# Log-and-exp roots, reordered vector work and full-array identity products in a one-core encoder layer

## What is computed

```python
def _rwkv7_step(S, inp):
    r, w, k, v, a, b = inp
    Sa = jnp.einsum('zbhvk,zbhk->zbhv', S, a)
    S = S * w[..., None, :] + Sa[..., :, None] * b[..., None, :] + v[..., :, None] * k[..., None, :]
    return S, jnp.einsum('zbhvk,zbhk->zbhv', S, r)
...
kk = kk / jnp.maximum(jnp.sqrt(jnp.sum(kk * kk, axis=-1, keepdims=True)), 1e-12)
...
yn = ((y - mu) * lax.rsqrt(var + GN_EPS)).reshape(B, T, C) * ln_g + ln_b
```

## Time and profile before

| | |
|---|---|
| median of three runs | 1827.98 us |
| the profiled execution, its own time | 1829.13 us |
| its span | 1827.3 us |
| TensorE busy | 1716.3 us, 94% |
| VectorE busy | 586.4 us, 32% |
| ScalarE busy | 353.9 us, 19% |
| GpSimd busy | 63.1 us, 3% |
| mean granted TensorE clock | 0.989 |

### The profile page before, as it was taken

How to read it: one execution, slowest core, us unless ns; L and a number is a source line. 1 busy time by engine, 2 the same in 40 slices (tenths; PEclk the granted TensorE clock), 3 DMA queues, 4 the chain that set the end, 5 groups by cost and what they waited for, 6 DMA issues and landing times.

```text
span 1827.3 us, 37340 instructions
## 1 busy us (share of the span) xinstructions
PE 1716.3 (94%) x16231; PEld 1096.9 (60%) x16231; DVE 586.4 (32%) x1302; ACT 353.9 (19%) x945; POOL 63.1 (3%) x97
## 2 busy tenths in 40 slices
PE   8999999988989999999899999999999999999997
PEld 7887888867777445676545545454544444544443
DVE  2001333578886201022132322313132222222234
ACT  2122222267665201023100000000000000000002
POOL 1000000000000000002000000000000000000000
PEclk9999999999999999999999999999999999999999
DMA  9933353200000844328799999999999999999993
GB/s 308 206 110 101 110 165 138 92 4 4 4 4 5 297 164 177 130 113 301 291 426 430 429 429 430 431 432 427 433 428 433 428 433 427 433 428 430 429 419 148
DMA packets 95843, 503.65 MB, mean 276 GB/s; under 512 B 37869, under 2 KB 42369, under 8 KB 76913
## 3 DMA queue, kind: packets, MB, share of 16 engines
q1 hardware_dynamic: 90872, 488.17, 66.6%
q0 software_dynamic: 4608, 13.08, 2.4%
q10 hardware_dynamic: 248, 0.65, 0.1%
HBM read 511.29 MB, written 4.23 MB: 282 GB/s over the span
## 4 chain that ended last, share of the span: by engine, by line
PE 69%; DMA 22%; DVE 6%; issue 2%; ACT 1%; DVEq 0%; POOL 0%; SPq 0%; POOLq 0%; ACTq 0%
PE ps L1550 14%; PE ps L2067 8%; PE ps L2191 8%; PE ps L2056 8%; DMA ring<-in_wd 7%; DMA ring<-in_wu 7%; DMA rest<-in_wu 7%; PE ps L1874 6%; PE ps L2075 4%; PE ps L1892 2%; PE ps L1943 2%; PE ps L1960 2%; PE ps L1901 2%; PE ps L2047 1%; PE ps L1763 1%
## 5 line engine op out<-in xcount | busy, mean ns | idle before, releaser
L1550 PE MATMUL ps<-wide,ring 128*128 128x256 f32 x1248 | 275.3, 379 | 1.2 <-PE ps L1550 0.9
L1550 PEld LDWEIGHTS ps<-wide,ring 128*128 128x128 f32 x1248 | 239.0, 195 | 39.7 <-issue 10.1
L1410 DVE TENSOR_TENSOR tokA<-tokA,ps 128x512 f32<-128x512 f32 x256 | 158.5, 681 | 100.5 <-PE ps L2075 100.5
L2067 PE MATMUL ps<-ring,wide 128*64 128x256 f32 x1512 | 172.6, 387 | 16.8 <-DMA ring<-in_wu 16.6
L2191 PE MATMUL ps<-ring,gg 128*64 128x512 f32 x768 | 175.4, 598 | 2.3 <-DMA ring<-in_wd 1.6
L2056 PE MATMUL ps<-ring,wide 128*64 128x256 f32 x1536 | 173.0, 383 | 2.4 <-DVE wide L1398 2.4
L1423 DVE SCALAR_TENSOR_TENSOR gg<-ps,tmp,gg 128x256 f32<-128x256 f32 x32 | 15.5, 484 | 477.5 <-PE ps L2067 477.5
L2067 PEld LDWEIGHTS ps<-ring,wide 128*64 128x64 f32 x1512 | 110.5, 140 | 76.7 <-DMA ring<-in_wu 21.8
L2056 PEld LDWEIGHTS ps<-ring,wide 128*64 128x64 f32 x1536 | 109.8, 138 | 56.8 <-DVE wide L1398 4.0
L2075 PE MATMUL ps<-wide,gg 64*128 64x512 f32 x512 | 135.3, 627 | 0.9 <-ACT wide L824 0.8
L2191 PEld LDWEIGHTS ps<-ring,gg 128*64 128x64 f32 x768 | 50.9, 136 | 120.7 <-issue 111.9
(11 more groups left out here) (376 smaller groups left out, 2064.5 us busy)
## 6 DMA issues: line engine op xcount, KB each, us to landing
ring<-in_wg SPq DMA_DIRECT2D x23, 4096.0 KB, 28.6
ring<-in_wu SPq DMA_DIRECT2D x23, 4096.0 KB, 31.0
ring<-in_wd SPq DMA_DIRECT2D x22, 4096.0 KB, 32.0
rest<-in_wd SPq DMA_DIRECT2D x8, 4096.0 KB, 30.5
ring<-in_w_in SPq DMA_DIRECT2D x7, 4096.0 KB, 15.5
rest<-in_wu SPq DMA_DIRECT2D x7, 4096.0 KB, 29.7
rest<-in_wg SPq DMA_DIRECT2D x7, 4096.0 KB, 29.6
ring<-in_w_out SPq DMA_DIRECT2D x4, 4096.0 KB, 17.4
```

Source lines behind the costliest of these rows:

```text
L1410: V.tensor_tensor(fin_part(t, h, n), fin_part(t, h, n), ps[:, banks[q][h], :], ALU.add).then_inc(S["added"], 1)
L1550: ins = mm(ps[0:rows_, m % 2, 0:T], lhs, hnT[:, k, :], start=k == 0, stop=k == KD - 1)
L2067: ins = mm(ps[CAP * h:CAP * h + CAP, 1, 0:T], xT[:, k, CAP * i:CAP * i + CAP], w[:, T * h:T * h + T], start=k == 0, stop=k == KD - 1)
```

## The change

The diff has four parts.

1. Every `1/sqrt(v)` becomes `exp(-0.5 * ln(v))` on ScalarE, two activations on the same table, which is loaded by hand (`log_and_exp`). VectorE's reciprocals and its steps `v/width + eps` fall away, and so do the table switches in the pairs, for the cross-attention and for the router.

```diff
             def key_norm(p):
                 act.wait_ge(S["rw_n2e"], p + 1)
-                A(ew[:, SQ], ew[:, SQ], ACT.Sqrt).then_inc(S["rw_nrm"], 1)
+                A(ew[:, SQ], ew[:, SQ], ACT.Ln).then_inc(S["rw_nrm"], 1)
+                act.wait_ge(S["rw_nrm"], 2 * p + 1)
+                A(ew[:, SQ], ew[:, SQ], ACT.Exp, scale=-0.5).then_inc(S["rw_nrm"], 1)
...
             def key_norms(p):
-                dve.wait_ge(S["rw_nrm"], p + 1)
-                dc.add(V.reciprocal(ew[:, SQ], ew[:, SQ]))
+                dve.wait_ge(S["rw_nrm"], 2 * p + 2)
...
             def inverse_std(p):
-                dve.wait_ge(S["rw_std"], p + 1)
-                dc.add(V.reciprocal(VAR, VAR))
+                dve.wait_ge(S["rw_std"], 2 * p + 2)
```

```diff
                 if not last:
-                    A(warm, warm, ACT.Sqrt)
+                    key_norm(p + 1)
...
-                    if n == 9:
-                        if not first:
-                            head_std(p - 1)
-                        if not last:
-                            key_norm(p + 1)
+                    if n == 9 and not first:
+                        head_std(p - 1)
...
-                if next_:
-                    A(warm, warm, ACT.Exp)
-                    act.wait_ge(S["rw_tte"], 4 * p + 1)
-                    for n in range(3):
-                        exponential(p + 2, n)
...
                 if next_:
-                    for n in range(3, 8):
+                    for n in range(8):
                         exponential(p + 2, n)
```

```diff
+                if not last:
+                    key_norms(p + 1)
+                    unit_keys()
+                    products_ar(p + 1, 0)
+                    products_bk(p + 1, 0)
+                    products_out(0)
                 if not first:
                     inverse_std(p - 1)
                     normed_head(p - 1)
-                if not last:
-                    key_norms(p + 1)
-                if not first:
                     gated(p - 1)
                 dc.add(V.tensor_copy(BNS, ew[:, BON]))
                 if not last:
-                    unit_keys()
                     bonus_terms(p + 1)
-                    products_ar(p + 1, 0)
-                    products_bk(p + 1, 0)
-                    products_out(0)
-
+                    products_ar(p + 1, 1)
+                    products_bk(p + 1, 1)
+                    products_out(1)
+
+                dve.wait_ge(S["rw_gnow"], p + 1)
...
-                if not last:
-                    dve.wait_ge(S["rw_gnow"], p + 2)
-                    products_ar(p + 1, 1)
-                    products_bk(p + 1, 1)
-                    products_out(1)
+                if next_:
+                    keys(p + 2)
```

```diff
+    c[:, ID + P:ID + P + CH] = c[:, ID:ID + CH]
...
-                    for e, r, q, o in tiles():
-                        ins = mm(ps[o, 2 * g + e, CH:P], ident[q, q], src[q, g, e, 1, :], start=False, stop=True)
+                    for e in range(2):
+                        same_or_other = cst[:, ID + CH * e:ID + CH * e + P]
+                        ins = mm(ps[:, 2 * g + e, CH:P], same_or_other, src[:, g, e, 1, :], start=False, stop=True)
```

More of the change, by code:

```diff
@@ L443, in _ @@
             pool.memset(warm, 1.0)
+            pool.memset(dprm[:, 38:39], EPS)
             pool.memset(praw[:, :, :], 0.0).then_inc(S["zeroed"], 1)
-            pool.memset(idle, 0.0).then_inc(S["idle_in"], 1)
+            pool.memset(idle, 0.0)
             pool.memset(raw[:, :, 0:1], 0.0)
@@ L592, in _ @@
             lora_out(CT - 1)
+            log_and_exp()
             def pt_out(i):
@@ L616, in exponential @@
                     act.wait_ge(S["rw_gnow"], p)
-                if n == 4 and not now:
+                if n == 0 and not now:
                     act.wait_ge(S["rw_prep"], p)
@@ L775, in _ @@
             rows_turned(7, 2)
-            act.wait_ge(S["var_done"], 5)
-            A(stat(3, 2), stat(3, 1), ACT.Sqrt).then_inc(S["std_done"], 2)
+            std(3, 4, "row_sum", 1)
             for n in ("m_sil", "m_ya", "r_ohtok"):
@@ L842, in _, with last_std @@
                 job(NE // 2 - 1, 1, last=True)
+            def last_std(t):
+                one = slice(t, t + 1)
+                act.wait_ge(S["row_sum"], t + 2)
+                A(stat(5, 2)[:, one], stat(5, 0)[:, one], ACT.Ln, scale=1.0 / D, bias=eps).then_inc(S["ln_done"], 1)
+                act.wait_ge(S["ln_done"], 7 + t)
+                A(stat(5, 2)[:, one], stat(5, 2)[:, one], ACT.Exp, scale=-0.5).then_inc(S["std_done"], 1)
             for i, (n, t, h) in enumerate(FIN):
@@ L863, in _ @@
             V = nc.vector
[L865 to L869 removed]
             def normed(n):
                 src, _, dst, _, _ = NORMS[n]
[L873 to L874 removed]
+                dve.wait_ge(S["std_done"], n + 1)
                 for b in range(TB):
@@ L882, in _ @@
             vals = rt[:, 516:708].rearrange("p (b e v) -> p b e v", b=2, e=NE)
-            def block_rstd(n, b, turn_):
-                one = slice(b, b + 1)
-                V.tensor_scalar(stat(n, 1)[:, one], stat(n, 0)[:, one], 1.0 / D, EPS, ALU.mult, ALU.add).then_inc(S["var_done"], 1)
-                dve.wait_ge(S["std_done"], turn_)
-                dc.link(V.reciprocal(stat(n, 2)[:, one], stat(n, 2)[:, one]))
             def turned(n):
@@ L900, in _ @@
                 one = slice(b, b + 1)
-                dve.wait_ge(S["sq_done"], b + 1)
-                V.tensor_scalar(stat(0, 1)[:, one], stat(0, 0)[:, one], 1.0 / D, EPS, ALU.mult, ALU.add).then_inc(S["first_var"], 1)
                 dve.wait_ge(S["first_std"], b + 1)
-                dc.link(V.reciprocal(stat(0, 2)[:, one], stat(0, 2)[:, one]))
                 V.tensor_scalar(tokB[:, b, :], tokA[:, b, :], stat(0, 2)[:, one], None, ALU.mult).then_inc(S[("first_hn", "hn_done")[b]], 1)
@@ L1181, in _ @@
             projected(20)
-            dve.wait_ge(S["ya_sq"], 3)
-            rstd(4, C, EPS, 1)
+            dve.wait_ge(S["std_done"], 1)
             for b in range(TB):
@@ L1260, in row_rstd @@
                 dve.wait_ge(S["sq_done"], 14)
-                dc.link(V.tensor_reduce(stat(3, 0), sqp.rearrange("p (b q) -> p b q", b=2), AX.X, ALU.add))
-                V.tensor_scalar(stat(3, 1), stat(3, 0), 1.0 / D, EPS, ALU.mult, ALU.add).then_inc(S["var_done"], 2)
-                dve.wait_ge(S["std_done"], 5)
-                dc.link(V.reciprocal(stat(3, 2), stat(3, 2)))
+                V.tensor_reduce(stat(3, 0), sqp.rearrange("p (b q) -> p b q", b=2), AX.X, ALU.add).then_inc(S["row_sum"], 1)
+                dve.wait_ge(S["std_done"], 4)
             def logits(b):
@@ L1493, in _ @@
             tr = nc.tensor.transpose
-            pe.wait_ge(S["idle_in"], 1)
+            pe.wait_ge(S["zeroed"], 2)
+            for _ in range(TINY):
+                mm(ps[0:32, 6, 0:1], idle[:, 0:32], idle[:, 0:1], start=True, stop=True)
             pe.wait_ge(S["x_in0"], 16)
```

82 lines of the change are left out of this document (38 added, 44 removed).

## The result

| | before | after |
|---|---|---|
| median | 1827.22 us (1826.15 to 1830.10, 4 runs) | 1893.74 us (1892.85 to 1894.28, 4 runs) |
| ratio, 95% interval | | 1.0356 [1.0342, 1.0371] |
| profiled execution, its span | 1829.13, 1827.3 us | 1894.28, 1892.5 us |
| mean granted clock | 0.989 | 0.990 |

The change makes the kernel 3.6% slower. The median rose by 66.5 us; the forecast was 82.

A forecast was written before the change was run, and what follows sets the result against it. Weight transfers pace the experts, so losses in the pairs, nearly balanced between TensorE and VectorE, reach the end. 103 - 18 - 2 - 1.5 = +81.5 us on the profiled 1829.1 us gave 1910.6, said as 1910 us; range 1882 to 1936 us.

The forecast's parts named there:

- What bounds the kernel: Weight transfers set the experts' pace; time won or lost in the pairs shifts them whole, reaching the end one to one.
- The identity step: In the pairs' ladder, full-array instead of quarter products: +0.66 us a step, 160 steps, 105.6 us in all.
- The merged step at 7: Identity step and full-array sum side by side save one pair of transitions, 0.35 us, in seven pairs: -2.5 us.
- TensorE's gaps: Idle "issue" time in and just behind the ladder, read as slow instruction supply: 18 of 21.3 us won.
- Behind the ladder: After the ladder in each pair: 1.9 us of waits for VectorE at L1800, plus gaps counted within the 21.3 us.
- VectorE's order: In the pairs, reciprocals go and operands hide in the longer ladder: -2 us; with the old ladder about 1 us a pair.
- ScalarE: Two table loads of 1.28 us a pair go, but both end before the next copy is due: nothing won.
- The small chains: First norm, first pair, router and last norm lose a VectorE step or a load each: -1.5 us together.
- the main case: The forecast itself, 1910 us: given 73% and 1893 to 1927 us.
- Loads only: Rival for the identity step: transitions are hidden by loads that go ahead, 1857 us; 9%.
- The gaps stay: Rival for TensorE's idle time: the 18 us aren't won, 1928 us, or 1952 with the upper step price; 13%.
- Faster: Rival in the ladder: instruction count decides, 1799 us; saving used up once a step costs 0.18 us more; 4%.

The follow-up runs named there:

- run 2: The kernel before with only the full-array identity step, roots and orders as before: 1893.83 us, ratio 1.0367 to the kernel before.
- run 1: The changed kernel with its identity step put back as four quarter products: 1821.18 us, ratio 0.9968 to the kernel before.
- run 12: run 1's kernel with VectorE's old order in a pair, leaving the new roots and ScalarE's new order: 1824.78 us, ratio 0.9982 to the kernel before.
- run 10: run 1's kernel with two table loads a pair put back on ScalarE at the old places: 1822.18 us, ratio 0.9974 to the kernel before.
- run 3: The changed kernel with the full-array identity products of two neighbouring groups standing together, half as many transitions: 1869.45 us, ratio 1.0228 to the kernel before.
- run 6: run 1's kernel with 8 more instructions, waits met long before, in each ladder step: 1904.93 us, ratio 1.0405 to the kernel before.
- run 7: The changed kernel with 8 more instructions, waits met long before, in each ladder step: 2009.76 us, ratio 1.0982 to the kernel before.
- run 8: run 1's kernel with the six middle pairs in a hardware loop: 1917.41 us, ratio 1.0475 to the kernel before.
- run 9: run 1's kernel with two reciprocals a pair put back on VectorE, into a place nothing reads: 1845.34 us, ratio 1.0104 to the kernel before.
- run 5: run 1's kernel with 128 moving columns in each square, 64 into unread columns, as many instructions: 1823.21 us, ratio 0.9971 to the kernel before.
- run 11: run 1's kernel without identity products in the ladder's last level, VectorE adding instead: 1816.53 us, ratio 0.9948 to the kernel before.

## Why the prediction was right, and where it was off

- **What bounds the kernel: right.** The experts were shifted whole (911.8 and 910.7 us), and what the pairs lost reached the end.
- **The identity step, +0.66 us: right.** It is 0.64 (105.6 us predicted, about 102 measured). The single terms differ, and cancel in part by luck: the transitions are 0.11 + 0.15 + 0.05 = 0.31 us instead of 0.15 + 0.20 + 0.05 = 0.40, and the products four times 0.11 = 0.44 us instead of 0.37, where the last was counted short. The merged step at 7 saves 0.28 us instead of 0.35.
- **TensorE's gaps, -18 of 21.3 us: the term that was mis-sized.** All of them went. And a gap costs more than the idle time that its row lists. At 480.19 the row says 1.34 us, but the last start before it is at 478.62, 1.57 us earlier, where neighbours start 14 ns apart: the 0.23 us for which the last instruction is listed as busy are lost as well, 0.2 us a gap. In the ladders the listed 18.0 us of L1758, L1766 and L1763 were worth about 24.
- **Behind the ladder: also mis-sized.** The prediction has 1.9 us at L1800 and, within the 21.3, the 3.3 us at L1784 and L1775. Measured are 9.4 us. Besides these 5.2 and the start-to-start cost of their gaps, TensorE's idle time at the state's chunks (L1817, L1831) fell from 4.9 to 3.0 us. Under 2 us aren't attributed.
- **VectorE's order: sign right, reason half right.** The wait at L1800 went, but it goes in run 2 too, with VectorE's old order, so the -2 us belong to the longer ladder; with the old ladder "about 1 us a pair" was too much: some 6 us for roots and order together (run 1), of which the roots take more than half (run 12).
- **ScalarE: right.** The loads cost nothing (run 10). The small chains, -1.5 us, weren't measured apart. Under the change little of it is seen: the pairs begin at 370.4 us instead of 370.3, and from the first product of the output projection to the first gate product it is 270.0 instead of 270.5.
- **The sum.** By the measured terms: 102 - 2 - 24 - 9 = +67 against +66.5 measured. The forecast of 1910 us lies 16 us too high: 3 are the steps, 13 the gaps and what stands behind the ladder, and the small chains and the reference nearly cancel. The result lies at the lower edge of the 1893 to 1927 us that the main case was given, and of its signs one missed: a pair takes 37.3 us and not 39 to 40. The full-array step, 0.70 us from the end of L1749's slot, the missing gaps, the chain and the expert stage came as said.
- **The rivals.** *Loads only* (1857) falls: run 3 shows a price of 0.30 us for a transition that leaves the products alone. *The gaps stay* (1928) falls: none is left in the ladder. *Faster* (1799) falls: half as many identity instructions did win more than was listed, but the step costs 0.64 us more than before, beyond its point of decision of 0.18. The lower clock didn't come in the change (1.00 from 420 us on; 0.96 from 380 to 420, where the kernel before has 0.97); it came in runs 6 to 9.

The largest piece of the forecast was priced from a place in the old trace where the same transition already stood, between the same shapes; that, and two errors of opposite sign, is why it held. The gaps were priced by a column that lists only a part of what they cost.

## What to carry to other kernels

Price a product over quarters of the array by start to start, not by its mean duration: four small products side by side can be nearly free where two full ones in their place hold the engine five times as long, of which each way to the whole array and back is 0.3 us, so gather full-array products of several steps if they must be there. Where a dense stretch shows "issue" gaps at every 256 instructions, more array work in the same instructions costs nothing until the gaps are full (run 5) and fewer instructions win (run 11); take the gaps from start to start, since the listed idle time is too small. An engine's new order and its lighter work can depend on each other (run 9): try them apart before keeping one.

## What was not expected

- TensorE's instructions arrive in blocks of 256 by a DMA queue, one in 3.5 to 4.0 us when the engine has run dry. The experts' hardware loop, 1200 to 1700 us, shows no packet of that queue, and the pair's body in a loop (run 8) shows 36 in 170 us. But in run 8 the experts' loop, the same code as before, shows 18 between 1200 and 1700 us; why isn't known.
- A wait that is an instruction of its own costs TensorE 0.04 us in run 7 and 0.07 in run 6 even where it is long met, at the clock's upper level, and with such waits the clock fell for whole stretches.
- Eight quarter instructions start within 0.11 us, 14 ns apart, also over long stretches. By the Trainium skill, "TensorE: Matmul & The Clock Gate" ("Wait — 56ns, not 53.3ns?"), about 25 ns would be the least from one start to the next; for products that take turns over the four quarters the measurement decides.
- Two reciprocals a pair, 3.5 us of VectorE's time, cost 3 us a pair and took the granted clock of the pairs to 0.89 in one stretch (run 9). How much of the 24 us is the clock and how much the wait wasn't taken apart.
